# A hybrid SSD, attention and expert-retrieval block: the second token tile's products of the first pass moved into the gather loop

## What is computed

```python
n1 = modulate(h, norm1_g, sh1, sc1)
z, xbc, dtf, dtb, qkv, gate_ssd, gate_na = jnp.split(n1 @ w_in, IN_OFFSETS, axis=-1)
y_ssd = ssd_branch(z, xbc, ...) @ w_ssd_br
y_na = neighbourhood_attention(q, k, v, na_rpb) @ w_na_br
mixed = jax.nn.sigmoid(gate_ssd) * y_ssd + jax.nn.sigmoid(gate_na) * y_na
h = h + g1 * (mixed @ w_out)
n2 = modulate(h, norm2_g, sh2, sc2)
# peer(n2, ...), per token and each of 8 heads:
q = n2 @ w_q;  s = q . sub_keys              # two halves of 128 keys
top, e = 16 best of the pair sums            # 16 experts per head, 128 per token
act = gelu(u[e] . n2)
h = h + g2 * sum(softmax(top) * act * v[e])
out = rms_norm(h, final_g)
```

## Time and profile before

| | |
|---|---|
| median of 3 runs | 4229.41 us (4226.95 to 4229.63) |
| profiled execution, first to last instruction | 4220.8 us |
| PE busy | 2887.4 us, 68% |
| DVE busy | 2590.8 us, 61% |
| POOL busy | 2105.5 us, 50% |
| moved by DMA | 1419.20 MB, 336 GB/s over the span |

### The profile page before, as it was taken

One profiled execution on the slowest core, in us unless ns is written; L12 is line 12 of the kernel. 1 busy time (PEld: TensorE's weight loads), 2 busy tenths in 40 slices (PEclk: granted clock), 3 DMA queues, 4 the chain that ended last, 5 costly groups with the idle time before them and its releaser, 6 DMA issues.

```text
span 4220.8 us, 39974 instructions
## 1 busy us (share of the span) xinstructions
PE 2887.4 (68%) x13051; PEld 1538.2 (36%) x13051; DVE 2590.8 (61%) x5393; ACT 819.4 (19%) x1840; POOL 2105.5 (50%) x2154
## 2 busy tenths in 40 slices
PE   5989897798766866875677767856767663333334
PEld 4867776554333532322344223323432230000000
DVE  4642447524777866546887664468876656766652
ACT  3323113421122310111233011122320110000000
POOL 1000304001466555556766555567665657777775
PEclk8999998899888988988788888877888885565567
DMA  7424764536999999999999999999999999999999
GB/s 193 70 63 147 215 205 136 176 113 224 371 399 392 394 390 405 401 402 403 388 400 386 404 406 406 401 396 386 398 382 404 407 403 404 398 409 408 395 409 357
DMA packets 518220, 1419.20 MB, mean 336 GB/s; under 512 B 67032, under 2 KB 137664, under 8 KB 516992
## 3 DMA queue, kind: packets, MB, share of 16 engines
q0 software_dynamic: 298768, 1086.75, 66.9%
q1 hardware_dynamic: 219248, 329.91, 22.3%
HBM read 1348.45 MB, written 68.04 MB: 336 GB/s over the span
## 4 chain that ended last, share of the span: by engine, by line
DMA 31%; DVE 14%; PE 11%; issue 10%; POOL 9%; ACT 1%; SPq 0%; DVEq 0%; ACTq 0%; POOLq 0%
DMA ring<-in_peer_u,idx 26%; DVE junkF L2476 6%; POOL ring L2296 4%; POOL ring L2303 4%; PE ps_l L1698 4%; DMA ring<-in_peer_v,idxT 3%; PE acc L2522 2%; PE ps_l L1892 1%; PE ps_l L1767 1%; DVE nmax L2024 1%; DMA score_scr<-st 1%; PE ps_l L1906 1%; PE ps_l L1878 1%; DVE st L2010 1%; DMA qs<-score_scr 1%
## 5 line engine op out<-in xcount | busy, mean ns | idle before, releaser
L2476 DVE CUSTOM_DVE_ANT_0 junkF<-ring,ps_n2F 128x1024 bf16<-128x1024 f32 x1024 | 1248.8, 1220 | 854.1 <-DMA ring<-in_peer_u,idx 750.7
L2303 POOL DMA_INDIRECT ring<-in_peer_u,idx x1024 | 1003.8, 980 | 1116.2 <-DVE dots L2476 701.3
L2522 PE MATMUL acc<-ring,spread 128*32 128x512 f32 x4096 | 718.0, 835 | 919.5 <-DMA ring<-in_peer_v,idxT 919.3
L2296 POOL DMA_INDIRECT ring<-in_peer_v,idxT x1024 | 994.0, 971 | 326.7 <-issue 303.4
L1698 PE MATMUL ps_l<-lane 128*128 128x512 f32 x1856 | 845.7, 610 | 48.5 <-DMA lane<-n_scr 22.1
L2522 PEld LDWEIGHTS acc<-ring,spread 128*32 128x32 f32 x4096 | 145.7, 136 | 1357.7 <-issue 1354.3
L1698 PEld LDWEIGHTS ps_l<-lane 128*128 128x128 f32 x1856 | 352.7, 195 | 518.2 <-issue 512.2
L1892 PE MATMUL ps_l<-lane 128*128 128x128 f32 (+1 forms) x832 | 143.3, 314 | 59.5 <-ACT lane L1932 59.4
L1938 ACT ACTIVATE st<-st,nmax 128x512 f32<-128x512 f32 x128 | 92.4, 722 | 414.5 <-DVE nmax L2024 414.3
L1892 PEld LDWEIGHTS ps_l<-lane 128*128 128x128 f32 (+1 forms) x832 | 116.8, 208 | 139.1 <-ACT lane L1932 117.9
L699 POOL MEMSET colmask<- 128x64 f32 x1 | 0.2, 157 | 327.5 <-POOLq L558 327.5
(11 more groups left out here) (339 smaller groups left out, 3975.8 us busy)
## 6 DMA issues: line engine op xcount, KB each, us to landing
lane<-in_w_in SPq DMA_DIRECT2D x18, 2048.0 KB, 19.9
lane<-in_peer_wq SPq DMA_DIRECT2D x16, 2048.0 KB, 19.0
w_z<-in_w_in SPq DMA_DIRECT2D x16, 1024.0 KB, 5.9
adaB<-in_w_ada SPq DMA_DIRECT2D x16, 1024.0 KB, 6.5
lane<-in_w_na_br SPq DMA_DIRECT2D x8, 2048.0 KB, 22.0
lane<-in_w_ssd_br SPq DMA_DIRECT2D x8, 2048.0 KB, 20.3
lane<-in_w_out SPq DMA_DIRECT2D x8, 2048.0 KB, 19.4
ring<-in_peer_u,idx POOLq DMA_INDIRECT x1024
```

The source lines that it names most:

```text
L2296: pool.indirect_dma_start(v_rows[:, nv % RV, :], None, a["peer_v"][0], bass.IndirectOffsetOnAxis(ap=idxT[:, m % 2, col:col + 1], axis=0)). ...
L2303: pool.indirect_dma_start(u_rows[:, n % RU, :], None, a["peer_u"][0], bass.IndirectOffsetOnAxis(ap=idx[:, i % RI, j:j + 1], axis=0)).then_ ...
L2476: nc.vector.tensor_tensor_reduce(out=junk[:, :], in0=u_rows[:, n % RU, :], in1=ps_n[:, :], scale=1.0, scalar=0.0, op0=ALU.mult, op1=ALU.ad ...
L2522: last = nc.tensor.matmul(acc[q * QUAD:(q + 1) * QUAD, cols], spread[:, m % 2, c0:c0 + QUAD], v_rows[:, nv % RV, cols], start=(g == 0 and ...
```

## The change

The job list of pass 0 is written out. Tile 0 goes alone through merge and prepare up to its first query block: y turns, na, ssd, mix turns, out, norm. Two products of tile 1, `na` 0 and 1, stand beside tile 0's norm. `FIRST2` stands behind tile 0's first score as before, with 56 jobs ahead of it and not 71. Everything else of tile 1 and the query blocks 1 to 3 of tile 0 is in the loop, now up to slot 58 (`FIRST_END`); pass 1 starts there and still ends at slot 244. The slots of `GAP` become fewer for all later passes.

The weight blocks of pass 0 are a fixed list of eleven, with `out` column half 1 in it twice (for tile 0 and for tile 1), where ten were loaded before. Each has a fixed place (`home_of`): the two old ones, three in the columns of the v ring, and one in those of the first four u rows. Four blocks instead of two are loaded ahead of the attention (`AT_START`), two when it has ended (`AT_CLOSE`), the rest each behind the last product of its place. The second y tile is loaded later, behind tile 0's y turns. POOL gets one wait more, ahead of the first v gather: on the last product with a block in the rings (`RING_MULS`).

```diff
+        def asked(b, t):
+            return ("mul", "q", b, t), ("turnq", b, t), ("score", b, t)
+        q_jobs = {(b, t): asked(b, t) for b in range(QW // HALF) for t in PASSES[0]}
-        first = attend(0) + merge(PASSES[0]) + prepare(PASSES[0])
+        first = attend(0) + rows_of("y", 0) + parts_of("na", 0) + parts_of("ssd", 0) + rows_of("mix", 0) + parts_of("out", 0)
+        first += [("norm1", 0), ("mul", "na", 0, 1), ("norm2", 0), ("mul", "na", 1, 1)] + rows_of("n2", 0) + list(q_jobs[0, 0])
+        first += [q_jobs[1, 0][0]] + rows_of("y", 1) + [q_jobs[1, 0][1], ("mul", "ssd", 0, 1), q_jobs[1, 0][2], ("mul", "ssd", 1, 1)]
+        first += rows_of("mix", 1) + parts_of("out", 1) + [("norm1", 1), q_jobs[2, 0][0], q_jobs[3, 0][0], q_jobs[2, 0][1], ("norm2", 1)] + rows_of("n2", 1)
+        first += [q_jobs[2, 0][2], q_jobs[3, 0][1], q_jobs[2, 1][0], q_jobs[3, 0][2], q_jobs[3, 1][0], q_jobs[2, 1][1], q_jobs[0, 1][0], q_jobs[2, 1][2],
+                  q_jobs[3, 1][1], q_jobs[1, 1][0], q_jobs[3, 1][2], q_jobs[0, 1][1], q_jobs[0, 1][2], q_jobs[1, 1][1], q_jobs[1, 1][2]]
...
+        FIRST_BLOCKS = [("na", 0, None), ("na", 1, None), ("ssd", 0, None), ("ssd", 1, None), ("out", 0, None), ("out", 1, 0),
+                        ("q", 0, None), ("q", 1, None), ("out", 1, 1), ("q", 2, None), ("q", 3, None)]
+        AT_START, AT_CLOSE = (0, 1, 2, 3), (4, 5)
+        home_of = [0, 1, 3, 4, 2, 5, 0, 1, 3, 4, 2]
...
+        homes = [w[:, r, :, :] for r in range(RW)]
+        homes += [ring[:, at:at + KD * HALF].rearrange("p (k n) -> p k n", k=KD) for at in [RU * DM + i * KD * HALF for i in range(3)] + [0]]
...
+        RING_MULS = max(number[block_last[blk]] for blk in range(len(FIRST_BLOCKS)) if home_of[blk] >= RW)
...
                 if it == ALL_UNITS[a_pass] + 3:
+                    if not a_pass:
+                        sp.wait_ge(o_done, ALL_UNITS[0])
+                        for blk in AT_CLOSE:
+                            load_block(sp, blk)
...
+            if kind == "turn" and JOBS[n][1:] == ("y", 0, 1):
+                load_tok(sp, 2)
...
-                for g in range(RT):
-                    load_tok(sp, g)
-                for blk in range(RW):
+                load_tok(sp, 0)
+                for blk in AT_START:
                     load_block(sp, blk)
...
-        FIRST_END, PASS_MARGIN = 14, 12
+        FIRST_END, PASS_MARGIN = 58, 12
         LATE_SLOTS = 8
-        GAP = dict(gate=10, sdec=LATE_SLOTS + 3, att=11, y=3, na=4, ssd=3, mix=2, n2=8, q=1)
+        GAP = dict(gate=8, sdec=LATE_SLOTS + 2, att=10, y=2, na=3, ssd=3, mix=2, n2=7, q=1)
...
                             if k == 0:
                                 pool.wait_ge(idxT_done, m + 1)
+                            if nv == 0:
+                                pool.wait_ge(p_mm, RING_MULS + 1)
```

More of the change, by code:

```diff
@@ L1614, in sp_job @@
                 blk = block_of[n]
[L1615 to L1616 removed]
+                follower = block_after(blk)
+                if n == block_last[blk] and follower is not None:
+                    first = min(k for k in block_of if block_of[k] == follower)
                     if not passes_between(n, first):
[L1618 removed]
+                        load_block(sp, follower)
                 if n in gin_of and gin_of[n] + RG < len(gin_jobs):
```

44 lines of the change are left out of this document (28 added, 16 removed).

## The result

The changed kernel takes 4281.22 us (median of 4 runs, 4278.01 to 4283.45), the kernel before 4229.52 in the same comparison (4226.95 to 4234.56): a ratio of 1.0117, with a 95% interval from 1.0101 to 1.0132. It is slower, and outside the predicted range of 4201 to 4240 us. The profiled execution spans 4281.5 us, before 4220.8. A run's time lies 2 us above its span here (4283.45 us for the one with 4281.5), so the span of 4220.8 belongs to an execution at the fast end of the kernel before: the two spans are 60.7 us apart, the two medians 51.7.

The account below looks back on a forecast made before the run. PE's chain bounds the kernel before the first gather, transferred bytes after it. Seam 974.7, first slots 100, rest 3129.5 and losses 9 gave a 4213 us span; with 8.6 added, 4221 us, range 4201 to 4240.

Parts of the forecast that it names:

- the pair: Attention: two more weight blocks queued on SP ahead of the fourth head pair's loads delay PE, +4 us, bounds 0 and +9.
- the first 45 slots: Loop slots 0 to 44, before the first v gather, take 100 us, bounds 95 and 108, with DVE pacing part.
- The chain before the seam: PE work before the first gather (the seam, 1020.33 us) gets shorter: seam to 970.7, -49.6 us, bounds -52 and -45.
- the 985 that I had named as the limit: Sign at the seam: the forecast is wrong if the first gather comes after 985 us; 970 to 980 was expected.
- The bytes: Behind the first gather: 8.65 MB of loads and stores now run there, +21.6 us at 400 GB/s.
- ring wait: Slot 45: POOL's new wait for the last product using v ring blocks costs 0, bound +8 us.
- The held ring: Rival: POOL waits in slot 45 for q(3,1) as late products run at 1.2 GHz; 4229 to 4237 us, chance 0.10.
- The squeezed second pass: Jobs of tiles 2 and 3 in slots 58 to 244 instead of 14 to 244: +9 us, bounds 0 and +46.
- the bound (+46): Second pass: upper bound if losses of attention, recurrence, gates, and merge and queries all come together; half was counted.
- The gaps: Passes 2 and 3: smaller gaps cost nothing, since loads take 20 us and gaps stay at 7 slots; bound +-3 us.
- The rival that came true: Second-pass attention keeps today's 5.26 us per iteration in 47 slots: 189.5 us instead of 160, +29.5, 4250 us, chance 0.15.
- its point of 4.9 us an iteration: Second-pass attention: over 4.9 us for each of 36 iterations (177 us), the result is slower than before by over 0.2%.

Follow-up runs that it names:

- e1_pairs_first: Changed kernel with the third and fourth weight block loaded behind the fifth head pair's loads, not ahead of the attention: 4266.0 us, ratio 1.0078.
- e9: Kernel before with second-pass jobs in slots 58 to 244, not 14 to 244, and DVE's dot products cut to 256 of 1024 columns (slots 89 to 243): 4268.0 us.
- e10: Kernel before with second-pass jobs in slots 58 to 244, and PE's v-row sums cut to 128 of each 512 columns (slots 89 to 243): 4278.3 us.
- e16: Kernel before with second-pass jobs in slots 58 to 244, and both DVE's dot products and PE's v-row sums cut (slots 89 to 243): 4255.8 us, ratio 1.0056.

## Why the prediction was wrong, step by step

The forecast span was 4213 us and the measured one 4281.5, 68 more. The first gather came at 991.12 instead of 974.7 us, 16.4 late (of which 10.9 are chance, 4.2 the pair and 1.0 the chain); the first 45 slots took 9.5 us more than forecast; from there to the end it was 3180.9 us instead of 3138.5, 42.4 more. For the median I had added 8.6 us to the span. A run's time lies 2 us above its span, and the other 6.6 were the scatter of a fast profiled execution. That error happened to lie on the side of the result: the median misses by 60 us and not by 67.

- **The chain before the seam (-49.6): right.** 141.1 us became 92.5, -48.6; with the pair's 8.2 and the 10.9 of chance on top, the first gather came at 991.12 instead of 974.7, outside the 985 that I had named as the limit, though the step itself held to 1 us.
- **The pair (+4, bounds 0 and 9): the mechanism right, the size near the upper bound.** 8.2 us, by e1_pairs_first. SP issued the pair's first load at 809.60 and not at 790.28 as in the earlier trace rows; 10.9 us of that are the later start of the tail, and the other 8.4 are the shift that I had put at 9.2. The mis-sized term is the landing, "some 5 us": the pair's last load was issued at 813.64, and PE went on at 823.47, 9.8 us later, while the two blocks ahead of it on the queue were still on their way (such a block took 20.2 us to land there, and the last was issued at about 802). That makes the product some 6 us late; 2 us more went in the attention behind it, which I did not follow.
- **The bytes (+21.6): right.** 1421.30 MB moved, as said. (The DMA row stands at 9 from slice 10 on and not from 13, as I read it; no term uses that.)
- **The first 45 slots (100 us, ring wait 0, bound +8): wrong.** 109.5 us, with a wait of 11.1. The step that failed is "eleven slots of 2.07 us are 22.8 us: it holds nothing". DVE's timeline of the changed kernel around tile 1's norm, the square sum that ends the first half, a dot product, and the second half:

```profile
1059.49 1.22 DVE L2099 CUSTOM_DVE_ANT_0 junkF<-lane 128x1024 bf16<-128x1024 f32 x1
...
1060.88 1.22 DVE L2523 CUSTOM_DVE_ANT_0 junkF<-ring,ps_n2F 128x1024 bf16<-128x1024 f32 x1
...
1075.41 0.16 DVE L2105 RECIPROCAL lstat<-lstat 128x1 f32<-128x1 f32 x1
...
1076.92 1.23 DVE L2112 TENSOR_TENSOR tok<-tok,shift 128x1024 f32<-128x1024 f32 x1
```

  The norm's sum was ready at 1060.9; its slot, 34, was reached by DVE at 1075.4, after ten dot products. A job waits for its slot on the slowest engine, not for its data. And DVE reaches a slot up to five after POOL, since the u ring has five places: POOL was ready for the first v gather at 1088.27, 10.1 us behind the norm's end at 1078.15, not 22.8. The two products and turns behind it took from 1078.30 to 1099.0, 21 us and not 17, partly at the lower clock (0.75 in slots 0 to 44): the two turns took 1.94 us, where the eight matmuls of such turns took 1.10 at 898.62. PE had nothing to do meanwhile; its longest waits:

```profile
1020.08 1.09 PE L1730 MATMUL ps_l<-ident,lane 128*128 128x128 f32 x4 [22.16 <-DVE lane L2136]
...
1078.30 1.94 PE L1730 MATMUL ps_l<-ident,tok 128*128 128x128 f32 x8 [15.89 <-DVE tok L2112]
```

  With the end at 46 the slots took 101.6 us, so some 8 of the 9.5 us are this wait (the edit moves the other jobs too). The held ring was a rival at 0.10, with 8 us; its mechanism was there, but the slow clock was the smaller part of it.
- **The squeezed second pass (+9, bounds 0 and +46): wrong, and the largest part of the miss, some 40 of the 68 us.** The squeeze alone cost 51 us by the ratio (47 by the medians). The gate stage was costed rightly at about nothing (2 us more unused in slots 45 to 88), and so were merge and queries (3.5 us in slots 181 to 243). The attention was put at 160 us for 47 slots (4.44 us an iteration) "at 95% PE"; it ran at 4.79 us an iteration in the change, its 47 slots took 175.2 us, and 23.5 us more than before went unused, where the forecast had +5. In the squeeze alone the iteration was nearly as forecast, 4.50, and the slots still lost 23.1 us more than before, so the iteration's length is not the whole of it. The recurrence was put at +2 (0 to 8), and slots 89 to 133 lost 16 us more than before, outside its bounds. What failed is the way of costing: I summed each engine's work, found it below the transfers' time, and took the transfers to be the limit. An engine at 77% (DVE, 134 of 175 us) and one at 83% (PE, 145) hold the transfers if their work alternates and both must do it in slot order; e9, e10 and e16 show that the slots' own work on both engines together is over half of it (24 of the 41 us that the squeeze adds in slots 89 to 180): in the attention neither engine alone, in the recurrence DVE. The cause of the rest stays open. I had the bound (+46) in my hand and counted half of it for the range; the four parts came together, 45 us by the unused time.
- **The gaps (at nothing, bounds +-3): wrong in the kernel before (+20 us), not measurable in the changed one.** "Loads take 20 us and the gaps stay at 7 slots of 3.1 us and more" looked at the loads that a gap covers. A gap may also be the time in which a lagging engine catches up; that was not tested, and why the gaps cost 20 us stays open.
- **The rival that came true** is the attention's, at 0.15, with 4250 and its point of 4.9 us an iteration. It is true in its direction only: the iterations stayed below that point, yet the result is worse than it said, since the recurrence lost as well and the first slots, the pair and the late tail came on top.

## What to carry to other kernels

Where a hand-written schedule feeds a saturated transfer, look at the rate by stage when a stage is given fewer slots: here engines at 80% that wait for one another in slot order were already the limit, and the first 22 of 44 slots taken from them cost 0.4%. Work moved into a loop with slots waits for its slot on the last engine, not for its data, so a chain of moved jobs must be costed in slots of that engine, and the places of a ring between it and the engine that issues come off the room. A gain at the seam must be weighed against what its jobs push aside, and that is tested by pushing alone, before the rest is built.

## What the hardware showed beside this

Executions of one kernel scatter by some 10 us to either side, from 4218.5 to 4243.3 us over 13 runs of the kernel before. Part of it arises early: the tail started at 760.63 us in the profile before and at 756.1 to 774.1 in the others, with the same instructions ahead of it. In both profiled executions, before and after, the DMA engines were 90% or more busy in most of 130 to 144 us while they moved 64 to 109 GB/s, and nearly all packets of 130 to 160 us are under 2 KB; the slowest 512 KB weight load of that time landed after 11.0 us before and after 30.9 in the change. So I compared stretches from a fixed event of each trace, not absolute times. The second surprise is the chip on which the same program takes 4.8% longer, with transfers at 319 to 370 GB/s in parts of the loop: a rearrangement that costs 0.32% on one chip gained 0.35% there.
